# Routing of an expert-choice encoder block: last tile's logits in token-major form, ranks as fp32r products, one selection instruction, one tile scaled by GpSimd

## The reference, cut to what matters

```python
h2 = _rmsnorm(x, g_ffn) * (1 + sc2) + sh2
logits = einsum('bsd,de->bse', h2, w_router)      # 512 tokens, 16 experts
aff = softmax(logits, axis=-1)
vals, idx = top_k(swapaxes(aff, 1, 2), cap)       # each expert takes cap = 64 tokens
xg = h2[idx]
y = (silu(xg @ w_e_gate) * (xg @ w_e_up)) @ w_e_down * vals
x = x + gt2 * scatter_add(y, idx)
```

## Time and profile before

| what | value |
|---|---|
| median of three executions | 2192.13 us |
| the profiled execution, its span | 2192.3 us |
| instructions | 26368 |
| TensorE matmul busy | 96% of the span |
| VectorE, ScalarE, GpSimd busy | 40%, 26%, 0% |
| HBM read | 621 MB |
| chain that ended last | TensorE 84%, DMA 12%, VectorE 2% |

### The profile page before, as it was taken

One profiled execution on the slowest core, in us unless ns is written; L12 is line 12 of the kernel. 1 busy time (PEld: TensorE's weight loads), 2 busy tenths in 40 slices (PEclk: granted clock), 3 DMA queues, 4 the chain that ended last, 5 costly groups with the idle time before them and its releaser, 6 DMA issues.

```text
span 2192.3 us, 26368 instructions
## 1 busy us (share of the span) xinstructions
PE 2110.8 (96%) x10319; PEld 1373.3 (63%) x10319; DVE 875.9 (40%) x1246; ACT 564.0 (26%) x998; POOL 4.7 (0%) x8
## 2 busy tenths in 40 slices
PE   7999999999999999999999899998999989998986
PEld 5787888888887777888888545353534444444432
DVE  4762667666676665346333301112020302021114
ACT  4263432222246664113222511010101110011102
POOL 0000000000000000000000000000000000000000
PEclk9999999999999999999999999999999999999999
DMA  9948675887760001533422799999999999999998
GB/s 364 385 162 297 231 259 200 318 305 280 281 231 25 25 1 57 178 131 128 164 87 87 309 392 408 426 426 428 427 427 427 428 428 427 427 428 427 426 422 308
DMA packets 144063, 634.81 MB, mean 290 GB/s; under 512 B 11986, under 2 KB 29544, under 8 KB 112756
## 3 DMA queue, kind: packets, MB, share of 16 engines
q1 hardware_dynamic: 139348, 625.38, 72.5%
q10 hardware_dynamic: 4640, 8.40, 1.0%
HBM read 621.15 MB, written 12.58 MB: 289 GB/s over the span
## 4 chain that ended last, share of the span: by engine, by line
PE 84%; DMA 12%; DVE 2%; ACT 1%; issue 0%; SPq 0%; DVEq 0%; ACTq 0%
PE bank L804 24%; PE bank L1311 23%; PE bank L806 13%; DMA e_wide<-in_w_e_up 10%; PE bank L1283 5%; PE bank L990 5%; PE bank L864 3%; PE bank L1083 3%; PE bank L1303 1%; PE bank L1071 1%; DMA e_slot<-in_w_e_down 1%; PE bank L1304 1%; PE bank L769 1%; PE bank L1293 1%; PE bank L1195 1%
## 5 line engine op out<-in xcount | busy, mean ns | idle before, releaser
L1311 PE MATMUL bank<-e_wide,xgT 128*64 128x512 f32 x1456 | 404.5, 606 | 42.7 <-DMA e_wide<-in_w_e_up 26.4
L1492 ACT ACTIVATE w_hi<-stage 128x1024 fp32r<-128x1024 f32 (+1 forms) x168 | 175.4, 1044 | 594.5 <-PE bank L804 339.8
L1918 DVE TENSOR_TENSOR w_lo<-stage,w_hi 128x1024 fp32r<-128x1024 f32 (+1 forms) x168 | 202.4, 1205 | 302.6 <-ACT w_hi L1492 302.0
L1311 PEld LDWEIGHTS bank<-e_wide,xgT 128*64 128x64 f32 x1456 | 130.8, 139 | 285.1 <-issue 284.2
L1311 PE MATMUL bank<-e_slot,xgT 128*64 128x512 f32 x584 | 207.0, 598 | 0.0
L1311 PE MATMUL bank<-e_wide,heT 128*64 128x512 f32 x672 | 167.4, 594 | 0.0
L804 PE MATMUL bank<-hT_hi,w_hi 128*128 128x512 f32 x512 | 159.1, 392 | 0.0
L804 PE MATMUL bank<-hT_lo,w_hi 128*128 128x512 f32 x512 | 157.9, 390 | 0.0
L804 PE MATMUL bank<-hT_hi,w_lo 128*128 128x512 f32 x512 | 157.7, 389 | 0.0
L2490 DVE TENSOR_TENSOR x<-x,bank 128x512 f32<-128x512 f32 x128 | 79.6, 682 | 191.8 <-PE bank L1304 190.3
L1993 DVE SCALAR_TENSOR_TENSOR ada_acc<-ada_tile,siluc,ada_acc 128x1024 f32<-128x1024 f32 x116 | 148.8, 1282 | 6.7 <-DMA ada_tile<-in_w_ada 1.0
(11 more groups left out here) (363 smaller groups left out, 2961.4 us busy)
## 6 DMA issues: line engine op xcount, KB each, us to landing
e_wide<-in_w_e_up SPq DMA_DIRECT2D x49, 2048.0 KB, 17.3
e_wide<-in_w_e_gate SPq DMA_DIRECT2D x42, 2048.0 KB, 15.1
e_wide<-in_w_e_down SPq DMA_DIRECT2D x42, 2048.0 KB, 17.2
ada_tile<-in_w_ada SPq DMA_DIRECT2D x156, 512.0 KB, 5.8
stage<-in_w_in SPq DMA_DIRECT2D x96, 512.0 KB, 6.6
e_slot<-in_w_e_gate SPq DMA_DIRECT2D x43, 1024.0 KB, 16.4
e_slot<-in_w_e_down SPq DMA_DIRECT2D x41, 1024.0 KB, 17.1
e_slot<-in_w_e_up SPq DMA_DIRECT2D x30, 1024.0 KB, 10.8
```

Source lines behind the costliest of these rows:

```text
L1311: last = mm(acc[h][64 * e:64 * e + 64, :], stationary(e), weights(h, e), start=first, stop=end)
L1492: A(w_hi[:, c % NSPLIT, :, 0:width], stage[:, c % NSTAGE, :, 0:width], ACT.Copy).then_inc(hi_ready, 1)
L1918: V.tensor_tensor(w_lo[:, c % NSPLIT, :, 0:width], stage[:, c % NSTAGE, :, 0:width], w_hi[:, c % NSPLIT, :, 0:width].bitcast(F32), ALU.sub ...
```

## The change

- The last tile's logits do not go through bank 6. TensorE multiplies tile_logits(2) before transpose_tile(3); the copy to logits_sb waits for the first three tiles only and moves ahead of the last sum of squares on ScalarE; the fold runs, and four products with h2T[3] as the stationary operand and 16 columns of w_rta as the moving one add the last tile's part in bank 4 directly. Two of the three rows_warm go. logit_done ends at 7 rather than 8, so that the value 7 now means "fold and last tile complete".
- `over` becomes fp32r; two new tiles tri_r and ones_r are copied by VectorE from tri and ones, after the 1/rms values and before the wait for the logits; the four rank products take these operands.
- select(p) is one VectorE instruction of 128x512 rather than four of 128x128.
- ScalarE scales tiles 0 to 2; GpSimd scales tile 3, one tensor_scalar of 128x2048, after its four diag tiles and the 1/rms values.

```diff
...
             def tile_logits(t):
-                if t < 3:
-                    pe.wait_ge(h2T_act, t + 1)
-                else:
-                    pe.wait_ge(h2T_ready, 13)
+                pe.wait_ge(h2T_act, t + 1)
...
             transpose_tile(2)
             tile_logits(1)
             rows_warm(1)
+            tile_logits(2)
             transpose_tile(3)
-            tile_logits(2)
-            rows_warm(1)
-            tile_logits(3)
-            rows_warm(1)
             pe.wait_ge(h2T_act, 4)
             for t in range(T):
-                last = mm(bank[4][:, t * NE:(t + 1) * NE], logits_sb[:, t * P:(t + 1) * P], fold4[:, :], start=True, stop=True)
+                mm(bank[4][:, t * NE:(t + 1) * NE], logits_sb[:, t * P:(t + 1) * P], fold4[:, :], start=True, stop=t < T - 1)
+            pe.wait_ge(h2T_ready, 13)
+            for i in range(4):
+                last = mm(bank[4][:, 3 * NE:T * NE], h2T[3][:, i * P:(i + 1) * P], w_rta[:, 12 + i, 0:NE], start=False, stop=i == 3)
             last.then_inc(logit_done, 1)
...
-            mm(bank[4][:, 0:P], tri[:, :], over[:, :, :, :], start=True, stop=False)
+            mm(bank[4][:, 0:P], tri_r[:, :], over[:, :, :, :], start=True, stop=False)
             for n in range(1, T):
-                last = mm(bank[4][:, 2 * NE * n:P], ones[:, :], over[:, 0:T - n, :, :], start=False, stop=n == T - 1)
+                last = mm(bank[4][:, 2 * NE * n:P], ones_r[:, :], over[:, 0:T - n, :, :], start=False, stop=n == T - 1)
...
-            for t in range(T):
+            for t in range(T - 1):
                 square_out(3, t)
-                if t < 3:
-                    act.wait_ge(h2T_done, 12 + t + 1)
-                    act.wait_ge(logit_done, 3)
-                    A(h2T[t][:, :], bank[4 + t % 2][:, :], ACT.Copy).then_inc(h2T_act, 1)
+                act.wait_ge(h2T_done, 12 + t + 1)
+                act.wait_ge(logit_done, 3)
+                A(h2T[t][:, :], bank[4 + t % 2][:, :], ACT.Copy).then_inc(h2T_act, 1)
+            act.wait_ge(logit_done, 6)
+            A(logits_sb[:, :], bank[6][:, :], ACT.Copy).then_inc(h2T_act, 1)
+            square_out(3, 3)
...
-            act.wait_ge(logit_done, 7)
-            A(logits_sb[:, :], bank[6][:, :], ACT.Copy).then_inc(h2T_act, 1)
...
-            for t in range(T):
+            for t in range(T - 1):
                 normalised(t)
...
             dve.sem_inc(rstd2_ready, 1)
-            dve.wait_ge(logit_done, 8)
+            dve.wait_ge(wr_in, 32)
+            V.tensor_copy(tri_r[:, :], tri[:, :])
+            V.tensor_copy(ones_r[:, :], ones[:, :])
+            dve.wait_ge(logit_done, 7)
...
-                for t in range(T):
-                    last = V.tensor_tensor(sel[:, t, :, :], iota[:, :].unsqueeze(1).broadcast_to([P, 2, CAP]),
-                                           slots[:, t, ds(2 * p, 2)].unsqueeze(2).broadcast_to([P, 2, CAP]), ALU.is_equal)
-                last.then_inc(sel_ready, 1)
+                V.tensor_tensor(sel[:, :, :, :], iota[:, :].unsqueeze(1).unsqueeze(1).broadcast_to([P, T, 2, CAP]),
+                                slots[:, :, ds(2 * p, 2)].unsqueeze(3).broadcast_to([P, T, 2, CAP]), ALU.is_equal).then_inc(sel_ready, 1)
...
+            pool.wait_ge(rstd2_ready, 1)
+            G.tensor_scalar(xn[:, 3, :].rearrange("q (k j p) -> q k j p", j=ROWS, p=P), x1[:, 3, :].rearrange("q (k p j) -> q k j p", p=P, j=ROWS),
+                            rstd[:, 15:16], None, ALU.mult).then_inc(xn2_ready, 1)
```

More of the change, by code:

```diff
@@ L186, in encoder_block @@
         tri = at("ada", 10 * KB, "tri", [P, P])
-        over = at("ada", 10 * KB + 512, "over", [P, T, 2, NE])
+        over = at("ada", 10 * KB + 512, "over", [P, T, 2, NE], F32R)
         limits = at("ada", 11 * KB, "limits", [NE, 2, P])
@@ L215, in encoder_block @@
         room = at("A", 4 * KB + 512, "room", [P, NE])
+        tri_r, ones_r = at("A", 5 * KB, "tri_r", [P, P], F32R), at("A", 5 * KB + 512, "ones_r", [P, P], F32R)
         e_slot = [at("ring", 8 * i * KB, f"e_slot{i}", [P, 2, 2 * W]) for i in range(6)]
@@ L1177, in tile_logits @@
             def tile_logits(t):
-                if t < 3:
-                    pe.wait_ge(h2T_act, t + 1)
-                else:
-                    pe.wait_ge(h2T_ready, 13)
+                pe.wait_ge(h2T_act, t + 1)
                 for i in range(4):
                     last = mm(bank[6][32 * i:32 * i + 32, t * P:(t + 1) * P], w_rta[:, 12 + i, :], h2T[t][:, i * P:(i + 1) * P],
-                              start=False, stop=t == T - 1)
+                              start=False, stop=t == T - 2)
                 last.then_inc(logit_done, 1)
@@ L2464, in _ @@
             link(V.tensor_tensor(place[:, :, :], ranks[:, :, 1, :], free, ALU.min))
-            V.tensor_tensor(keep[:, :, :], keep[:, :, :], over[:, :, 1, :], ALU.mult)
+            V.tensor_tensor(keep[:, :, :], keep[:, :, :], over[:, :, 1, :].bitcast(F32), ALU.mult)
             link(V.tensor_tensor(place[:, :, :], ranks[:, :, 0, :], place[:, :, :], ALU.add))
-            link(V.tensor_tensor(keep[:, :, :], keep[:, :, :], over[:, :, 0, :], ALU.add))
+            link(V.tensor_tensor(keep[:, :, :], keep[:, :, :], over[:, :, 0, :].bitcast(F32), ALU.add))
             link(V.tensor_tensor(slots[:, :, 0:NE], place[:, :, :], keep[:, :, :], ALU.mult))
             def select(p):
-                for t in range(T):
-                    last = V.tensor_tensor(sel[:, t, :, :], iota[:, :].unsqueeze(1).broadcast_to([P, 2, CAP]),
-                                           slots[:, t, ds(2 * p, 2)].unsqueeze(2).broadcast_to([P, 2, CAP]), ALU.is_equal)
-                last.then_inc(sel_ready, 1)
+                V.tensor_tensor(sel[:, :, :, :], iota[:, :].unsqueeze(1).unsqueeze(1).broadcast_to([P, T, 2, CAP]),
+                                slots[:, :, ds(2 * p, 2)].unsqueeze(3).broadcast_to([P, T, 2, CAP]), ALU.is_equal).then_inc(sel_ready, 1)
             def y_scaled(p, jd, chunks):
```

## The result

The changed kernel takes 2198.3 us (median of 15, 2196.48 to 2199.56), the kernel before 2193.66 us on the same chips (median of 15, 2192.0 to 2196.12). The ratio is 1.002, with a 95% interval of 1.0013 to 1.0027: 4.6 us slower. The forecast was 2192.5 us, within 2190.0 to 2195.5. The profiled execution has a span of 2197.2 us, where that of before had 2192.3.

What follows compares the result with a forecast made beforehand. TensorE was taken to lead the weight stream up to 1367 us, so the first gather's shift reaches the end. VectorE's wait, nearly repaid by logits, ranks, selection and full clock, gave 2192.3 + 0.4 - 0.2 = 2192.5 us, range 2190.0 to 2195.5.

Steps and rivals of the forecast that it cites:

- What bounds the kernel: Expert weight stream: loads wait for slots and slots for TensorE until 1367 us, so the first gather's shift reaches the end.
- The rival by which the change does not reach the end: The weight stream's start at 1219.7 alone sets the end, whatever the routing does: 2192.1 us; chance 0.07.
- Logits: Last tile's logits added directly in bank 4: VectorE could start on them at 1224.5, 0.8 us earlier.
- GpSimd's tile: GpSimd's scaling of tile 3 takes 4.1 us and holds VectorE's two-SBUF-operand sum, which moves 2.9 us later.
- TensorE's clock at the ranks: Clock falls early in a 3.9 us idle stretch, returns, and is full at the ranks; if low, gather 2.0 us later.
- The ranks: Four rank products in fp32r rather than fp32: saves half of 2.01 us, leaving 1.0 us at half clock, 0.6 at full.
- The selection: One VectorE instruction of 128x512 takes 0.69 us where four pieces cost 0.90; saves 0.2 us in pair 0.
- The sum: First gather at 1243.1 against 1242.91, 0.2 us later, plus up to 0.3 for held copies; 2.0 later at low clock.
- The slower rival: GpSimd's tile takes 7.6 us and VectorE waits for all of it: 2195.6 to 2197.5 us; chance 0.10.
- No waiting: VectorE does not wait for GpSimd's tile beyond what the old trace shows: 2190.6 us, between 2189.5 and 2191.4; chance 0.23.

Runs made afterwards that it cites:

- x4_plain_read: Changed kernel, but GpSimd reads and writes tile 3 in plain order (output not the reference's): 2197.59 us, one run, against 2194.9 for the kernel before.
- z3_psum_shift: Changed kernel, but VectorE's sum with the shift reads the shift row from PSUM: 2197.7 us, one run, against 2193.62 for the kernel before.
- y1_before_tile: Kernel before with only GpSimd's scaling of tile 3 added (ScalarE scales three): 2197.15 us, one run, against 2193.62 for the kernel before.
- x2_tile_later: Changed kernel, but GpSimd's tile waits until the affinities are done: 2193.34 us against 2194.9 for the kernel before, ratio 0.9993.
- z1_warm_early: x2_tile_later with five filler products, not two, behind the third round of max and none behind the ranks: 2193.11 us against 2193.62 for the kernel before.
- x1_act_tile: Changed kernel, but ScalarE scales all four tiles and GpSimd none: 2193.79 us against 2194.9 for the kernel before, ratio 0.9997.

## Why the prediction was wrong, point by point

**What bounds the kernel: right.** The table's first expert product and the load behind the gap move together, within 0.02 us, in all eleven other kernels, from 3.56 us earlier to 4.43 later. From that load to the end it is 825.2 to 826.2 us in all of them. The rival by which the change does not reach the end falls in both directions, as far as the traces go.

**Logits: right.** The sum with the shift was due 0.93 us earlier where 0.8 was worked out. The clock has a say even here: the removed rows_warm were costed at nothing, as TensorE waited there, and in some executions the clock fell right behind this stretch (at 4.6 to 5.2 in five kernels, all without them). But it did not in five others with the same products there. Whether the rows matter for it was not tried.

**GpSimd's tile: the mechanism right, the size wrong.** This term of the sum was mis-sized. The prediction took 4.1 us from the diag products, with 2.1 and 7.6 as ends; the tile took 7.28 us. The nearest row was of another operation and a quarter of the length, and the step of four elements, which the upper end priced by ScalarE's factor, was there to see in the code. Of the 3.2 us missed, 1.8 is the step (x4_plain_read), and the rest the engine's rate on this operation. The prediction also held VectorE until the tile's end. The sum ends 1.64 us before that, 5.64 us after the tile's start. The prediction has it end about 4.5 us after the start: 4.1 for the tile, 0.2 until the sum begins and 0.23 for the sum. So the term was short by 1.1 us. The copies to tri_r and ones_r were not held by the tile: both stand ahead of the sum, and the first took 0.60 us beside the last diag product.

The Trainium skill (SBUF — State Buffer, "Who interferes with whom") says that a VectorE instruction with two SBUF inputs and a GpSimd instruction that reads SBUF shut each other out. The changed kernel and z3_psum_shift agree, with 5.22 and 4.71 us. It also says that an instruction with at most one such input, outside the modes that use both ports, is not held: L2423, max and replace beside the tile agree. Of the modes that use both ports it says that the pair is held for the whole instruction; the prediction read this for two inputs too, but here the held instruction ends 1.64 or 1.65 us before GpSimd's record does, in all five tiles. The skill (GPSIMD Engine Reference, "Performance pitfalls for Q7 kernels") gives about 2.9 cycles an element for this step. That is 4.95 us, an estimate from its figure; 7.28 us were measured, and the measurement decides.

**TensorE's clock at the ranks: wrong.** The prediction expected it to fall in the long idle stretch (it had fallen before that, at 1224.3, while TensorE was at work on gate_rows), to come back in time (it did, at 1234.6), and to stay through the next idle stretch. It fell at 1241.4, just as the ranks began, after 3.4 us in which TensorE had no product and two small transposes of 0.23 us. This is the step that failed by most. The prediction had 2.4 us of idle time there, which leaves TensorE some 6.9 us of work from the affinities' transposes to the end of the filler. It was 6.1: the clock came back 3.4 us after TensorE had begun again, not 6, so the filler ran at full clock, in 1.98 us, as soon as the third round of max let it go. So the stretch up to the thresholds was 3.4 us long. It is just as long in the kernel before, where the clock fell as well:

```profile
1236.65 0.28 PE L1270 MATMUL bank<-ident,limits 16*128 16x16 f32 x1 [3.43 <-DVE limits L2448]
```

The filler's start and the thresholds both hang on VectorE's rounds, so a longer or shorter hold moves the stretch and does not change it: it is 3.4 us in y1_before_tile and x2_tile_later too. So filler and gather cost 1.8 and 1.0 us more than at full clock. The ranks took 1.13 us at the low clock against 1.0 worked out, and 0.71 at full clock in z1_warm_early against 0.6. The selection took 0.69 us, as its row said.

**The sum.** Forecast 0.2 to 0.5 us later at full clock, 2.0 at low clock. To these 2.0 come 1.1 for the hold, 0.2 for the affinities' transposes and 0.1 for the ranks, and 1.0 for the gather at the low clock, which the prediction left out in this case: 4.4 us, where the first expert product shows 4.43 and the medians 4.6. Between the forecast of 0.2 and this the clock has about 3 us and the hold 1.1. x4_plain_read shows it from the other side: there the sum ends 3.8 us after the tile's start, sooner than the prediction had it, and the first expert product is still 2.42 us late, at the low clock. The slower rival, 2195.6 to 2197.5, with a tile of 7.6 us and the low clock, was given 0.10. The measured loss lies in it, partly by luck: its hold was about 2.2 us too long, and it left the gather's 1.0 us out. The low chance was an error of judgement all the same: the price of GpSimd's tile and the clock at the ranks were the least known terms of the sum, and the chances were spread as if both were known.

**No waiting** (0.23) fell. x1_act_tile and x2_tile_later show what it would have given: 0.7 to 1.1 us at the first expert product, about the 0.9 that the prediction worked out for a clock that comes back at its old time.

## What to carry to other kernels

Before work goes to GpSimd, list what VectorE does meanwhile: a VectorE sum or difference with two operands in SBUF stood still for most of GpSimd's instruction here, while max, replace, a reduction and instructions with an operand in PSUM ran on beside it. Place the work beside those. Price a GpSimd instruction by its own operation, length and step, and not by another's. And where several engines are ready within a microsecond or two of each other, look at the clock before you price a shorter chain. Here a gain of 2.0 us at the selection was worth 0.7 to 1.1 us at the first expert product, and filler products in both idle stretches, in front of the ranks and behind them, brought the earliest one.

## What the runs showed of the hardware

GpSimd's tensor_scalar on fp32 takes 3.36 ns an element with a read step of four elements, beside 0.40 us once (7.28 and 3.84 us for 2048 and 1024 elements), and by the same 0.40 us 2.5 ns in plain order (5.47 us). The held VectorE instruction ends 1.64 or 1.65 us before GpSimd's record does, at tiles of 3.84, 5.47 and 7.28 us. The routing differs by some 1.6 us between z3_psum_shift and the changed kernel by the clock, with a hold that is the same to 0.01 us. The clock fell behind the same products in the traces of five kernels and not in those of five others, and four of these ten run the same instructions well beyond that point. So the kernel's instructions alone do not decide it; what does was not tried.
